# One of six weight subtractions per step moved from VectorE to GpSimd in a routed expert layer

## What is computed

```python
def moe_swiglu(x, w_router, w_gate, w_up, w_down):
    logits = (x @ w_router).astype(jnp.float32)
    top_val, top_idx = lax.top_k(logits, TOP_K)
    top_w = jax.nn.softmax(top_val, axis=-1)
    gate = ...            # top_w put in the chosen experts' columns
    for e in range(N_EXPERTS_2):
        h = jax.nn.silu(x @ w_gate[e]) * (x @ w_up[e])
        y = y + gate[..., e:e + 1] * (h @ w_down[e])
```

## Time and profile before

| | |
|---|---|
| median of 3 runs | 2724.12 us (2719.31 to 2725.2) |
| the profiled execution | 2715.65 us, of which the span from first to last instruction 2713.9 us |
| PE busy | 2454.3 us, 90% of the span |
| DVE busy | 1425.4 us, 53% |
| ACT busy | 1142.2 us, 42% |
| POOL busy | 113.6 us, 4% |
| the second routed layer | from about 1627 us to 2695 us of the span |
| L2036, subtractions of the layer | 336, 2.29 us each |

### The profile page before, as it was taken

One profiled execution on the slowest core, in us unless ns is written; L12 is line 12 of the kernel. 1 busy time (PEld: TensorE's weight loads), 2 busy tenths in 40 slices (PEclk: granted clock), 3 DMA queues, 4 the chain that ended last, 5 costly groups with the idle time before them and its releaser, 6 DMA issues.

```text
span 2713.9 us, 29339 instructions
## 1 busy us (share of the span) xinstructions
PE 2454.3 (90%) x11580; PEld 1886.5 (70%) x11580; DVE 1425.4 (53%) x1661; ACT 1142.2 (42%) x1299; POOL 113.6 (4%) x88
## 2 busy tenths in 40 slices
PE   5998697899799888999989978999999999999995
PEld 4884576333377577997765666778787878778784
DVE  0004424022203646761017446888888888888885
ACT  1114312111121424431015336767676767676762
POOL 4000300000000002220000000000000000000000
PEclk9997898999999898999859988999999999999997
DMA  9540042799853033566310026989999999999992
GB/s 223 161 153 3 1 140 93 314 415 416 324 154 109 8 101 114 187 203 185 81 62 1 32 93 257 362 323 350 337 352 331 351 332 350 331 351 332 326 354 112
DMA packets 285608, 592.00 MB, mean 218 GB/s; under 512 B 12351, under 2 KB 117967, under 8 KB 277184
## 3 DMA queue, kind: packets, MB, share of 16 engines
q1 hardware_dynamic: 279728, 571.48, 59.4%
q0 software_dynamic: 5776, 19.11, 2.5%
HBM read 589.44 MB, written 1.11 MB: 218 GB/s over the span
## 4 chain that ended last, share of the span: by engine, by line
PE 80%; DMA 7%; ACT 5%; DVE 5%; issue 3%; POOL 0%; SPq 0%; DVEq 0%; ACTq 0%
PE psB L930 9%; PE psF L916 8%; PE psF L917 8%; PE psF L918 8%; PE psF L1033 5%; PE psB L916 5%; PE psB L917 5%; PE psB L918 5%; PE psB L937 4%; DMA ring<-in_w_dram 3%; PE psF L1044 3%; PE psB L1079 3%; DMA ring<-in_moe_w_gate_dram 3%; PE psF L1206 2%; PE psB L1228 2%
## 5 line engine op out<-in xcount | busy, mean ns | idle before, releaser
L2036 DVE TENSOR_TENSOR ring_rounded<-ring,arena_rounded 128x2048 fp32r<-128x2048 f32 x224 | 507.6, 2288 | 90.7 <-ACT arena_rounded L1600 90.7
L1600 ACT ACTIVATE arena_rounded<-ring 128x2048 fp32r<-128x2048 f32 x224 | 431.0, 1924 | 178.4 <-DMA ring<-in_moe_w_down_dram 124.9
L917 PE MATMUL psF<-ring_rounded,arena_rounded 128*128 128x512 f32 x896 | 355.9, 397 | 0.0
L930 PE MATMUL psB<-hT,ring 128*128 128x256 f32 x928 | 212.3, 392 | 5.7 <-ACT hT L1481 5.7
L930 PEld LDWEIGHTS psB<-hT,ring 128*128 128x128 f32 x928 | 182.5, 198 | 34.0 <-ACT hT L1481 7.3
L917 PEld LDWEIGHTS psF<-ring_rounded,arena_rounded 128*128 128x128 f32 x896 | 170.7, 191 | 36.3
L916 PE MATMUL psB<-arena_rounded,PT_rounded 128*128 128x512 f32 x448 | 180.8, 404 | 14.7 <-DVE PT_rounded L2041 14.6
L918 PE MATMUL psB<-arena_rounded,PT_rounded 128*128 128x512 f32 x488 | 193.4, 396 | 0.0
L916 PE MATMUL psF<-arena_rounded 128*128 128x512 f32 x448 | 177.7, 397 | 2.9 <-ACT arena_rounded L1622 1.5
L917 PE MATMUL psB<-ring_rounded,PT_rounded 128*128 128x512 f32 x448 | 177.9, 397 | 0.0
L918 PE MATMUL psF<-arena_rounded 128*128 128x512 f32 x448 | 175.9, 393 | 0.0
(11 more groups left out here) (347 smaller groups left out, 4258.4 us busy)
## 6 DMA issues: line engine op xcount, KB each, us to landing
ring<-in_moe_w_gate_dram SPq DMA_DIRECT2D x112, 1024.0 KB, 5.0
ring<-in_moe_w_up_dram SPq DMA_DIRECT2D x112, 1024.0 KB, 5.0
ring<-in_moe_w_down_dram SPq DMA_DIRECT2D x112, 1024.0 KB, 4.9
ring<-in_w_dram SPq DMA_DIRECT2D x96, 1024.0 KB, 8.9
ring<-in_w_in_dram SPq DMA_DIRECT2D x14, 1024.0 KB, 5.1
ring<-in_ff_w_gate_dram SPq DMA_DIRECT2D x11, 1024.0 KB, 7.3
ring<-in_ff_w_up_dram SPq DMA_DIRECT2D x11, 1024.0 KB, 9.8
ring<-in_ff_w_down_dram SPq DMA_DIRECT2D x11, 1024.0 KB, 5.0
```

The lines of the kernel that those rows point to most:

```text
L917: mm(bank, x1, w2, start=False, stop=False)
L930: last = mm(bank[:, T * j:T * j + T], wt[:, k, P * j:P * j + P], x[:, k, :], start=(k == 0), stop=(k == kt - 1))
L1600: ap_(w_hi[slot].bitcast(R32), ring[:, slot], ACT.Copy).then_inc(q["high"], 1)
L2036: V.tensor_tensor(ring_r[:, slot].bitcast(R32), ring[:, slot], w_hi[slot], ALU.subtract)\
```

## The change

One list of chunk indices, `by_pool`, names chunk 4, the first down chunk of a step. GpSimd gets a loop over the layer's steps that waits for ACT's high part of chunk 4 and subtracts, counting on a new semaphore `low_pool`. DVE leaves chunk 4 out. PE waits for chunk 4 on `low_pool` and for the other five on `low_dve`. Tiles, transfers and the matmuls are as before.

```diff
+        self.by_pool = [4]
+        self.by_dve = [i for i in self.every if i not in self.by_pool]
...
+            def low_round(layer, r):
+
+                q = layer.q
+
+                def low(n, i, where):
+                    slot = (layer.first + i) % RING
+                    pool.wait_ge(q["high"], layer.nth(layer.every, r, n, i, where))
+                    nc.gpsimd.tensor_tensor(ring_r[:, slot].bitcast(R32), ring[:, slot], w_hi[slot], ALU.subtract)\
+                        .then_inc(q["low_pool"], 1)
+
+                def unit(u, begin, end):
+                    for s in range(layer.per):
+                        first_step = begin and s == 0
+                        for i in layer.by_pool:
+                            if not (first_step and i >= 4):
+                                low(u * layer.per + s, i, "first" if first_step else "in")
+
+                experts_loop(nc.gpsimd.Fori, layer, unit)
+                low(layer.n, 4, "last")
+
+            def routed_layer(layer):
+                low_round(layer, 0)
+                pool.wait_ge(counted, 2)
+                crowded_rounds(nc.gpsimd, layer, lambda r: low_round(layer, r))
+
...
             for n in range(7, 10):
                 load_gb(n)
+            routed_layer(layers["moe2"])
...
-                    pe.wait_ge(q["low_dve"], layer.nth(layer.every, r, n, i, where))
+                    if i in layer.by_pool:
+                        pe.wait_ge(q["low_pool"], layer.nth(layer.by_pool, r, n, i, where))
+                    else:
+                        pe.wait_ge(q["low_dve"], layer.nth(layer.by_dve, r, n, i, where))
...
                     if layer.split and not begins:
-                        low(n, 4)
                         low(n, 5)
                         turned(n)
...
                 if layer.split:
-                    low(layer.n, 4, "last")
                     low(layer.n, 5, "last")
                     turned(layer.n)
```

More of the change, by code:

```diff
@@ L375, in two_block_kernel @@
             layer.q = {k: sem(f"{name}_{k}") for k in (
-                "tokens_act", "tokens_dve", "picked", "gathered", "rows_saved", "slots_ready", "slots_act", "slots_dve", "high", "low_dve", "used",
+                "tokens_act", "tokens_dve", "picked", "gathered", "rows_saved", "slots_ready", "slots_act", "slots_dve", "high", "low_dve", "low_pool", "used",
                 "silu", "hidden", "turned", "turned_act", "turned_dve", "marked", "marks_saved", "y_act", "y_dve", "scattered", "shifted",
```

## The result

| | before | after |
|---|---|---|
| median | 2722.16 us (2719.31 to 2725.2, 4 runs) | 2761.06 us (2753.07 to 2766.18, 4 runs) |
| ratio to before | | 1.0138, 95% interval 1.0111 to 1.0165 |
| the profiled execution | 2715.65 us, span 2713.9 | 2753.07 us, span 2751.3 |
| DVE busy | 1425.4 us | 1390.6 us |
| POOL busy | 113.6 us | 379.1 us |

The changed kernel is 1.38% slower by the ratio, 38.9 us between the medians and 37.4 between the two profiled executions. Each of these is faster than its kernel's median, the one before by 6.5 us and the one after by 8.0.

The account below looks back on a forecast made before the run. PE was taken to bound the layer. Losses of 8.7 (ordinary steps), 14.1 (scatter), 1.6 (unit 0) and 3.2 us (end) summed to 27.6, on the median of the runs shown 2724.1 + 27.6 = 2752 us, range 2731 to 2773.

Parts of the forecast that it names:

- Bound of the layer, and no value in VectorE's relief: In the changed layer PE bounds; the 128 us of subtractions DVE loses are not on the path.
- GpSimd's pass and its start: Chunk 4 in each step: GpSimd starts 0.07 us after ACT's high part and takes 4.63 us.
- Exclusion for the whole pass: GpSimd's chunk 4 keeps DVE's chunk 5 out for its whole length; chunk 5 ends 2.15 us after it.
- Rival 2: DVE's subtraction of chunk 5 runs beside GpSimd's at full speed, so not slower: 2722 us, chance 0.10.
- Rival 3: Faster: DVE's earlier end gives PE back the 17.6 us of waits at the scatter: 2706 us, chance 0.04.
- Ordinary steps: Four steps in each of units 1 to 7: period 17.44 instead of 17.13 us, 28 x 0.31 = 8.7 us lost.
- Scatter: s = 1 of units 1 to 7: the hidden rows' split comes 2.02 us late with PE waiting, 14.1 us in all.
- a sign of being wrong: The prediction is wrong if PE falls out of the 2.4 GHz level in the longer scatter waits; no size given.
- Step with the gather: s = 6: the hidden rows' split ends at 2016.91, while PE is in the gather until 2018.36; nothing lost.
- Unit 0: It has no scatter, so s = 1 to 5 count as ordinary: 5 x 0.31 = 1.6 us lost.
- End: The layer's last two steps: down starts 1.4 us late in the last but one, 1.8 in the last, sum 3.2.
- Rival 4: Much slower: chunks 2 and 3 delay GpSimd up to 1 us, ordinary steps lose 1.3 each: 2780 us, chance 0.08.

Follow-up runs that it names:

- f1: Kernel before, all six subtractions on VectorE; ScalarE's turned put ahead of the next chunk 0, VectorE's turned ahead of chunk 5 except in gather steps: 2688.58 us, ratio 0.9875.
- the dummy: Kernel before plus one GpSimd subtraction of the same shape per step, on constants into a free tile, nobody waiting for it: 2822.9 us, ratio 1.037.

## Why the prediction was right, and where its sizes were off

It forecast a loss of 27.6 us through one mechanism, and the loss is 37.4 in the profiled execution, 2761 us against 2752 forecast. The mechanism held. The sizes were low nearly everywhere, and the total looks closer than they were: the part of the program ahead of the layer, which the change doesn't touch, came out 5.4 us shorter in the profiled execution after, so the layer itself lost some 43. The starts of the transposes of each step (L1237 before, L1268 after), added up, show where:

| from transposes to transposes | forecast | measured |
|---|---|---|
| unit 0, s = 1 to s = 6, 5 steps | 1.6 | 2.2 |
| s = 0 to 1, 7 | 0 | 0.1 |
| s = 1 to 2, with the scatter, 7 | 14.1 | 17.9 |
| s = 2 to 6, ordinary, 28 | 8.7 | 11.0 |
| s = 6 to 0, with the gather, 7 | 0 | 8.0 |
| the last two downs and the end | 3.2 | 3.6 |

Point by point:

- **Bound of the layer, and no value in VectorE's relief.** Right. The run without any subtraction of chunk 4 shows it alone: ratio 1.0014.
- **GpSimd's pass and its start.** Forecast 4.63 us and 0.07 after the high part; measured 4.63 from 2103.63, 0.08 after 2103.55.
- **Exclusion for the whole pass, chunk 5 ending 2.15 us after GpSimd.** Right to the hundredth, 2108.26 to 2110.41, and 2.15 to 2.16 in all 56 steps. Rival 2, that it runs beside, is out; so is the reading that only a two-port mode is held, for the rows show it for a plain subtraction. The prediction had also read the Trainium skill's page Advanced Engine Details and Errata too narrowly: its section Mode Summary tells of that mode alone, but its section GPSIMD Details names VectorE instructions with two SBUF inputs too, and the trace agrees (4.20 us recorded where 2.29 is usual). Rival 3, that the waits at the scatter go, is out too: they grew.
- **Ordinary steps.** Forecast a period of 17.44 and a loss of 0.31. In the step shown above, from down to down it is 2111.07 - 2093.36 = 17.71. The chain behind the high part was right; the way from down's start to the next high part was taken from before as 9.93 and is 2103.55 - 2093.36 = 10.19. Over one unit the starts of turned for s = 3 to 6 lie 17.70, 17.60, 17.66 and 17.59 us apart, where before they were 17.16, 17.14, 17.06 and 17.08: 0.5 a step. Over all 28 steps the starts of turned give 13.0 us and PE's transposes 11.0, instead of 8.7. Some 0.11 of the missing quarter microsecond is PE's own: a matmul that follows a wait is recorded with 0.50 us instead of 0.39, and the next starts 0.33 to 0.34 behind it instead of 0.23. Down waited in 24 places in all, not in over 30.
- **Scatter.** Forecast 2.02 us each; in the step shown PE's wait grew from 2.37 to 4.31, 1.94, and over seven by 12.0, where 14.1 was forecast. Yet these steps lost 17.9. The 5.9 between are the clock, a term that the sum doesn't have: from the scatter's first matmul to the next transposes the seven units took 128.8 us instead of 122.9, and 16.5 each, 115.3 in all, where the clock stayed up as in f1. The prediction named this as a sign of being wrong and gave it no price; it came true, and it had been there before the change too, in five of seven units.
- **Step with the gather.** Forecast nothing. This step of the argument failed. That turned has slack there is right, but what stands behind turned in VectorE's queue is late as well, and `slots`, which the next gate needs, is the last of it: 5.8 us at six gates, where 0.3 was before. Behind the longest of these waits the clock fell to 0.5 too, and the way from the gate to the transposes took 7.2 us instead of 5.6. These steps lost 8.0 in all. The prediction asked who waits for the held instruction and not who waits for the rest of its queue.
- **s = 0.** Forecast nothing, and nothing it was: its turned follows that of s = 6 by 20.11 us against 20.23 before.
- **Unit 0.** Forecast 1.6. From the layer's first transposes to its first scatter it is 169.4 us against 161.2, of which 2.0 are the scatter's: about 6. Some 3.3 of these are the next unit's first gate, its wait of 1.97 us instead of 0.31 and the 1.6 of the clock behind it, which are told above with the gather; the five steps themselves lost 2.2.
- **End.** From the last but one scatter to the last, 123.4 us against 119.4: 4.0, forecast 4.4 with the ordinary steps of that unit.
- **Rival 4**, GpSimd's pass kept waiting by chunks 2 and 3 in ordinary steps: not so, it starts at once and runs 4.61 to 4.66 us there. It does happen in the run with turned ahead of chunk 5, up to 6.2 us.
- **The unit.** Forecast 3.3 us more; from scatter to scatter, over six units, it is 134.0 us against 129.2, 4.9 more.

## What to carry to other kernels

Before work is moved from VectorE to GpSimd, look at what VectorE runs beside it: if both read SBUF and VectorE's instruction has two inputs there, nothing is overlapped, and what stands behind the held instruction in the queue pays. The same work cost 38 us in one place of the step and nothing that the medians show one chunk later, where the neighbour reads PSUM. When an instruction is delayed, follow its whole queue to the next one that somebody waits for, and ask of the releaser that is last, here ScalarE's order, before relieving one that is not. And when TensorE's waits change, look at the granted clock just behind them: here its fall behind the scatter's wait took 6 us more with the change and gave back 7 in f1, and a mean over a unit (0.99 both times) doesn't show it.

## What the runs showed of the hardware that was not expected

- The hold is the same both ways. A held VectorE pass ends its own length less 0.14 us after the end of GpSimd's, and a held GpSimd pass its own length less 0.15 to 0.19 us after VectorE's: 4.44 to 4.48 instead of 4.63 in six steps with the scatter of the kernel after, 3.46 instead of 3.65 with the dummy.
- GpSimd's subtraction of 128x2048 numbers took 4.51 us at least from two tensors, 3.65 at least with the same tensor as both inputs. Why was not tried.
- GpSimd's clear of 128x2048 numbers takes 1.81 us and runs beside VectorE's two-input pass with no loss to either, while a one-column subtraction, 0.19 us at least, is recorded with up to 2.37 us when it waits for the end of that pass.
- TensorE's granted clock fell to 0.5 for a few us behind five of PE's seven waits at the scatter before (2.4 to 3.1 us), and behind or already in all seven after (4.0 to 4.5 us). Two waits of 2.5 us before had no such fall; why was not tried.
